# MLA heads: probabilities times values as three rounded products instead of one plain fp32 product

## The chip, the cores and the metric

The kernel runs on one core of a Trainium2 chip. The metric is the device time of one execution in microseconds (us); times in a trace count from the start of the profiled span. The engines are PE (TensorE, its weight loads as PEld), DVE (VectorE), ACT (ScalarE), POOL (GpSimd) and SP (SyncE, which only issues DMAs here). Each works through its own instructions in order; semaphores tie them together.

## What is computed

Two blocks over 1024 tokens at a width of 1024, all in fp32. The first block is not touched. The second has two layers, each with a pooling branch and an attention branch (MLA); the latter is what changes. Cut to that, with L = 1040 (16 learned tokens in front) and 8 heads:

```python
q = (c_q @ w_q_b).reshape(B, L, N_HEADS, QK_HEAD_DIM)
kv = (c_kv @ w_kv_b).reshape(B, L, N_HEADS, QK_NOPE_DIM + V_HEAD_DIM)
...
s = jnp.einsum('bqhd,bkhd->bhqk', q[:, q0:kend], k[:, :kend]).astype(jnp.float32) * scale
s = jnp.where(valid, s, MASK_VALUE)
p = jax.nn.softmax(s, axis=-1).astype(v.dtype)
outs.append(jnp.einsum('bhqk,bkhd->bqhd', p, v[:, :kend]))
```

## The kernel before

Activations lie transposed in SBUF, features on partitions and 1044 (padded) tokens along the free dimension, in 9 key tiles of 128. Large products are made of rounded fp32 (fp32r) operands: each operand is split into a high part, its rounded value, and a low part, what is left, and three products are added (high times high, high times low, low times high). POOL splits the weights as they stream in (L353, L362), DVE the activations.

The MLA heads take two stretches, 1868 to 2207 us for layer 0 and 2867 to 3205 for layer 1. The order is written out by hand: every engine runs the same loops, `for h in range(-1, MH)` over heads and `for n in range(NB)` over 15 slots, and does in slot n what its own code says ("slot 5" below means n = 5). PE works on head h (scores, products with values) and on the projections of head g = h + 1; iteration -1 has projections only, the last (h = 7) none.

- The queries fall into three pieces of 384, 384 and 276 columns (`pc`), the work of a head into 15 blocks (`BLOCKS`): 0 and 1 for the first piece, 2 to 6 for the second, 7 to 14 for the third. A block is one key tile by all queries of its piece, or two tiles (256 + 128, or 148 + 20 columns) at a diagonal. By width: seven blocks of 384, seven of 276, one of 168; 18 tiles per head.
- `scores(h, n)` (L803, mask L807): three rounded products per tile into one of two banks. It waits until the exponents of block n - 2 are done.
- `exponents(h, n)` on ACT (L1307): one instruction per block from PSUM into a ring of PRING = 6 plain fp32 slots, `prob(k)`, in `work`. A slot is free when the product that read it is done.
- `weigh_values(h, n - 2)` at the end of slot n on PE (L824): values (128 x 128, half of the columns ones, which gives the sums of the probabilities too) times probabilities, plain fp32, accumulated in `aux`. The profile shows a plain fp32 product as two matmuls.
- For the next head on PE: `key_value_part` (L692, slots 0, 5, 10), `query_part` (L708), `key_sum` (L720), `turn_values` (L741, slots 3, 8, 13), `query_sum` (L730, slots 4, 9, 14). All but query_part use one PSUM bank, `acc_n`, and wait until its last reader is through (`n_free`). ACT reads it in `key_value_evict` (L1238), `key_scale` (L1264), `values_in` (L932, slots 4, 9, 14; it copies the turned values out) and `query_scale` (L1275, slots 5, 10, and 0 of the next head).
- On DVE: `maximum` (L1846) takes row maxima of rough scores (PE L757 with mask L761, two banks in turn), `maxima_of` (L1851, or L1853 and L1854) joins them and `turn_maxima` on PE (L778, slots 0, 5, 10) turns them; `query_table` (L1812 to L1814, slots 4, 9, 14), `key_norm` (L1834 to L1838, slots 5, 10, and 0 of the next head) and `query_norm` (L1822 to L1826, slots 6, 11, and 1) make and split keys and queries. `rough_scores` of the next head (first in slots 7 and 12) need the query's high part from L1825. `head_out` (L1863, L1864, slots 3, 6, 10) scales the output.
- DVE sets up the ones beside the values ahead of the first head (L1869, L1870). In the last head it splits two finished rows (L1416, L1417, slots 7 and 8).

## Time and profile before

| | |
|---|---|
| median of 3 runs | 3358.72 us (3355.52 to 3359.7) |
| profiled execution | 3356.4 us, its span 3354.6 us |
| PE busy | 3057.1 us (91%), 16352 matmuls |
| DVE busy | 1440.9 us (43%) |
| ACT busy | 694.5 us (21%) |
| POOL busy | 1074.3 us (32%) |
| PE L803, scores | 864 matmuls, 208.4 us busy |
| PE L824, values | 576 matmuls, 177.3 us busy |
| ACT L1307, exponents | 240, 104.2 us busy |

Matmuls are pipelined and their busy times overlap; what a product takes of the time is read from the chain of waits, which follows the work back from the end and gives each piece of time to one instruction. In a timeline, brackets hold the time that the engine was idle before the instruction and who released it; "issue" is a release that the profile can't name.

### The profile page before, as it was taken

The numbers are of one execution on the slowest core, as the hardware profiler recorded it, in microseconds if no ns is written. First come the engines' busy times: TensorE is split into PE (matmuls) and PEld (weight loads), VectorE is DVE, ScalarE is ACT, GpSimd is POOL, SyncE is SP. The second block draws the span as 40 slices with busy tenths as digits, with TensorE's granted clock in tenths as the row PEclk, the third lists the DMA queues.
The fourth block names the chain that finished last, engine by engine and source line by source line (L and its number), as shares of the span: only waits on it lengthen the run. The fifth ranks groups of instructions, "written<-read, shape, count | busy, mean of one in ns | idle before, by whom it ended". The sixth has DMA issues, their size and how long they took to land.

```text
span 3354.6 us, 41151 instructions
## 1 busy us (share of the span) xinstructions
PE 3057.1 (91%) x16352; PEld 2688.7 (80%) x16352; DVE 1440.9 (43%) x1730; ACT 694.5 (21%) x1239; POOL 1074.3 (32%) x1335
## 2 busy tenths in 40 slices
PE   6976678899999997799999899989899999999999
PEld 4754556677788775699999788889899999788889
DVE  4678454422222223830011666671820111766661
ACT  2132320000000001100111455510100110455500
POOL 3523013344444443333333211133433432211132
PEclk9988789999999998899999999999899999999999
DMA  2101011111111111211212000051211212000042
GB/s 104 44 32 35 1 63 39 49 46 44 50 44 47 47 44 44 77 51 45 102 45 83 32 14 14 14 185 45 89 51 45 96 51 77 32 16 18 15 178 76
DMA packets 46429, 182.50 MB, mean 54 GB/s; under 512 B 5968, under 2 KB 6096, under 8 KB 45776
## 3 DMA queue, kind: packets, MB, share of 16 engines
q1 hardware_dynamic: 31248, 113.19, 10.6%
q10 hardware_dynamic: 15040, 67.28, 5.3%
q8 instruction: 107, 1.75, 0.2%
q14 instruction: 34, 0.28, 0.0%
HBM read 150.06 MB, written 30.39 MB: 54 GB/s over the span
## 4 chain that ended last, share of the span: by engine, by line
PE 80%; DVE 13%; ACT 3%; issue 2%; POOL 1%; DMA 0%; DVEq 0%; ACTq 0%; POOLq 0%; SPq 0%
PE acc L425 59%; PE aux L824 4%; PE acc L708 4%; PE acc L803 3%; DVE act_lo L1417 2%; PE acc L757 2%; PE acc L692 1%; DVE residual L1482 1%; DVE work L1433 1%; DVE work L1426 1%; PE acc L778 1%; DVE act_hi L1416 1%; PE acc L720 1%; POOL w_lo L353 1%; DVE residual L1505 1%
## 5 line engine op out<-in xcount | busy, mean ns | idle before, releaser
L425 PE MATMUL acc<-act_hi,w_hi 128*128 128x348 f32 (+1 forms) x3104 | 770.6, 349 | 100.7 <-DVE act_lo L1417 41.2
L353 POOL TENSOR_TENSOR w_lo<-w_raw,w_hi 128x256 fp32r<-128x256 f32 (+1 forms) x924 | 817.3, 916 | 17.2
L425 PE MATMUL acc<-act_lo,w_hi 128*128 128x348 f32 (+1 forms) x3104 | 763.9, 346 | 0.0
L425 PEld LDWEIGHTS acc<-act_hi,w_hi 128*128 128x128 f32 x3104 | 546.3, 191 | 162.4 <-issue 68.1
L425 PE MATMUL acc<-act_hi,w_lo 128*128 128x348 f32 (+1 forms) x3104 | 618.8, 345 | 0.0
L425 PEld LDWEIGHTS acc<-act_lo,w_hi 128*128 128x128 f32 x3104 | 548.8, 190 | 43.1
L425 PEld LDWEIGHTS acc<-act_hi,w_lo 128*128 128x128 f32 x3104 | 530.0, 189 | 42.1
L373 POOL TENSOR_TENSOR small<-shape_consts 128x1 f32<-128x1 f32 x192 | 40.9, 213 | 1607.0 <-PE acc L425 1607.0
L425 PE MATMUL acc<-ff_split,w_hi 128*128 128x512 f32 (+1 forms) x1408 | 317.7, 375 | 11.9 <-DVE ff_split L1417 11.9
L1634 DVE TENSOR_TENSOR residual<-acc,residual 128x1024 f32<-128x1024 f32 (+1 forms) x88 | 108.1, 1228 | 473.0 <-PE acc L425 472.9
L425 PEld LDWEIGHTS acc<-ff_split,w_hi 128*128 128x128 f32 x1408 | 253.0, 188 | 60.8 <-DVE ff_split L1417 16.5
L362 POOL CAST w_hi<-w_raw 128x1024 fp32r<-128x1024 f32 x23 | 25.8, 1122 | 632.6 <-PE acc L708 544.4
L1846 DVE TENSOR_REDUCE small<-acc 128x1 f32<-128x512 f32 (+4 forms) x240 | 132.1, 550 | 192.5 <-PE acc L761 121.9
L803 PE MATMUL acc<-ff_split 128*128 128x276 f32 (+5 forms) x864 | 208.4, 354 | 0.0
L374 POOL CAST w_hi<-w_raw 128x1024 fp32r<-128x1024 f32 x192 | 202.5, 1055 | 0.0
L824 PE MATMUL aux<-work 128*128 128x276 f32 (+5 forms) x576 | 177.3, 404 | 0.0
L425 PE MATMUL acc<-ff_split,w_lo 128*128 128x512 f32 (+1 forms) x704 | 166.8, 374 | 0.0
L803 PEld LDWEIGHTS acc<-ff_split 128*128 128x128 f32 x864 | 140.8, 190 | 31.3 <-ACT work L1307 0.5
L1138 ACT ACTIVATE work<-acc 128x1024 f32<-128x1024 f32 x32 | 32.7, 1027 | 627.0 <-PE acc L425 626.4
L932 ACT ACTIVATE work<-acc 64x384 f32<-64x384 f32 (+5 forms) x153 | 93.5, 620 | 289.2 <-PE acc L425 255.7
L1307 ACT ACTIVATE work<-acc 128x384 f32<-128x384 f32 (+2 forms) x240 | 104.2, 435 | 233.9 <-PE acc L803 160.6
L425 PEld LDWEIGHTS acc<-ff_split,w_lo 128*128 128x128 f32 x704 | 127.2, 188 | 22.5
(228 smaller groups left out, 3307.6 us busy)
## 6 DMA issues: line engine op xcount, KB each, us to landing
w_raw<-in_wstream SPq DMA_DIRECT2D x215, 512.0 KB, 3.5
spill_x<-residual ACTq DMA_DIRECT2D x2, 4176.0 KB, 12.2
spill_m<-residual ACTq DMA_DIRECT2D x2, 4176.0 KB, 12.6
spill_g<-work ACTq DMA_DIRECT2D x16, 522.0 KB, 2.7
residual<-spill_m ACTq DMA_DIRECT2D x16, 522.0 KB, 6.1
work<-spill_g ACTq DMA_DIRECT2D x16, 522.0 KB, 8.6
residual<-spill_x ACTq DMA_DIRECT2D x16, 522.0 KB, 4.3
residual<-in_xT ACTq DMA_DIRECT2D x8, 512.0 KB, 9.9
```

Of the source, the lines that this page charges most:

```text
L353: ins = nc.gpsimd.tensor_tensor(Wl[:, s, c0:c0 + w], Wraw[:, s, c0:c0 + w], Wh[:, s, c0:c0 + w].bitcast(F32), ALU.subtract)
L374: nc.gpsimd.tensor_copy(Wh[:, s, :], Wraw[:, s, :]).then_inc(sems["w_hi_done"], 1)
L425: ins = nc.tensor.matmul(acc[0:m, s, p, 0:w], wt[:, ws, w0 + j * m:w0 + j * m + m], x[:, k, p * w:p * w + w], start=(first and t == 0), st ...
L708: ins = nc.tensor.matmul(acc_q[:, 0:w], wt[:, w_head[0], j * P:j * P + P], x[:, j, c0:c0 + w], start=(j == 0 and t == 0), stop=(j == 5 and ...
L757: ins = nc.tensor.matmul(acc_r[bank][:, 0:n], qh[:, min(P * i, LASTQ):min(P * i, LASTQ) + P], kh[:, 512 * p:512 * p + n], start=True, stop ...
L803: ins = nc.tensor.matmul(out, k2[kt][:, c0:c0 + P], q2[qt][:, lo:lo + w], start=m == 0, stop=(m == 2 and not diag))
L824: ins = nc.tensor.matmul(aux[:, b % 2, lo - QP * pc:lo - QP * pc + w], values(h)[:, t, :], prob(k)[:, at:at + w], start=t == 0, stop=end)
L932: return nc.scalar.activation(out, in_, ACT.Copy, scale=scale)
L1307: do(nc.scalar.activation(prob(k)[:, 0:w], src, ACT.Exp), "p_in")
L1417: do(vec.tensor_tensor(lo, src, hi.bitcast(F32), ALU.subtract), name)
L1634: do(vec.tensor_tensor(x, acc_view(s, pieces), x, ALU.add), f"free{s}")
L1846: do(vec.tensor_reduce(S_[:, col:col + 1], acc_r[rough_bank(i, p)][:, 0:n], AX, ALU.max, negate=True), "rough_max")
```

## The change

- Probabilities and values move from `work` to rounded tiles (`pool_split`), each in two parts. The ring has 4 slots (PRING) instead of 6.
- ACT takes each exponent twice from the same scores: in fp32 into the slot of the low part (`prob32`), and rounded into the high part. The signal `p_hi` comes after the second.
- DVE subtracts the two (`low_probabilities`, block n - 1 at the start of slot n) in place over the fp32 value, and forms the low part of the values from PSUM (`low_part_values`, slots 4, 9, 14), which ends the use of the bank `acc_n` (`v_lo` in place of `v_in`, in `turn_values` too).
- PE makes three rounded products per tile instead of one plain one. It waits for `p_lo`; `scores` waits for `p_hi`.
- DVE clears the low parts beside the ones ahead of the first head (two more instructions per value buffer).

The diff, without the list of semaphores and two renamed waits on PE:

```diff
@@ -178,22 +178,27 @@
 
 
 
-        PRING = 6
+        PRING = 4
         QP = 3 * P
         NQP = -(-TP // QP)
 
-        def values(h):
-
-            o = 8 * RW + TB * P * (h % 2)
-            return R_[:, o:o + TB * P].rearrange("p (t c) -> p t c", c=P)
-
-        ring0 = 2 * TB * P
-
-        def prob(k):
-            o = 8 * RW + ring0 + QP * (k % PRING)
+        def values(h, part):
+
+            o = TB * P * (2 * (h % 2) + part)
+            return G_[:, o:o + TB * P].rearrange("p (t c) -> p t c", c=P)
+
+        ring0 = 4 * TB * P
+
+        def prob(k, part):
+            o = ring0 + QP * (2 * (k % PRING) + part)
+            return G_[:, o:o + QP]
+
+        def prob32(k):
+
+            o = 8 * RW + ring0 + QP * (2 * (k % PRING) + 1)
             return R_[:, o:o + QP]
 
-        idr0 = ring0 + QP * PRING
+        idr0 = ring0 + 2 * QP * PRING
         ident_r, causal_r, after_r = (G_[:, idr0 + P * i:idr0 + P * i + P] for i in range(3))
         extra0 = idr0 + 3 * P
         assert extra0 + QP <= 8 * RW
...
@@ -788,7 +793,7 @@
                     k = block_no(l, h, n)
                     pc, tiles = BLOCKS[n]
                     if k > 2:
-                        pe.wait_ge(sems["p_in"], k - 2)
+                        pe.wait_ge(sems["p_hi"], k - 2)
                     if tiles[0][0] == 0:
                         pe.wait_ge(sems["max_row"], wave(l, h, pc))
                         pe.wait_ge(sems["k_lo"], wave(l, h, pc))
...
@@ -816,13 +821,15 @@
                     if tiles[0][0] == 0:
                         if b > 2:
                             pe.wait_ge(sems[f"av_free{b % 2}"], (b - 1) // 2)
-                        pe.wait_ge(sems["v_in"], b)
-                    pe.wait_ge(sems["p_in"], k)
+                        pe.wait_ge(sems["v_lo"], b)
+                    pe.wait_ge(sems["p_lo"], k)
                     at = 0
                     for t, lo, w in tiles:
                         end = n in ENDS and t == tiles[-1][0]
-                        ins = nc.tensor.matmul(aux[:, b % 2, lo - QP * pc:lo - QP * pc + w], values(h)[:, t, :],
-                                               prob(k)[:, at:at + w], start=t == 0, stop=end)
+                        for m, (v, part) in enumerate(((0, 0), (0, 1), (1, 0))):
+                            ins = nc.tensor.matmul(aux[:, b % 2, lo - QP * pc:lo - QP * pc + w],
+                                                   values(h, v)[:, t, :], prob(k, part)[:, at:at + w],
+                                                   start=(t == 0 and m == 0), stop=(end and m == 2))
                         at += w
                     ins.then_inc(values_done(l, h, n)[0], 1)
 
...
@@ -1279,14 +1286,14 @@
 
                 def values_in(g, pc):
 
-                    v1 = values(g)
+                    v1 = values(g, 0)
                     act.wait_ge(sems["v_turned"], wave(l, g, pc))
                     if pc < NQP - 1:
                         do(copy(v1[:, 3 * pc:3 * pc + 3, 0:64],
-                                acc_n[:, 0:192].rearrange("p (t v) -> p t v", v=64)), "v_in")
+                                acc_n[:, 0:192].rearrange("p (t v) -> p t v", v=64)), "v_hi")
                     else:
                         do(copy(v1[:, 6:8, 0:64], acc_n[:, 0:128].rearrange("p (t v) -> p t v", v=64)))
-                        do(copy(v1[:, 8, 0:64], acc_n[:, 128:192], param("rows20")), "v_in")
+                        do(copy(v1[:, 8, 0:64], acc_n[:, 128:192], param("rows20")), "v_hi")
 
                 def maximum_row(h, pc):
 
...
@@ -1304,7 +1311,8 @@
                     if k > PRING:
                         back = k - 1 - PRING
                         act.wait_ge(*values_done(back // (NB * MH), back // NB % MH, back % NB))
-                    do(nc.scalar.activation(prob(k)[:, 0:w], src, ACT.Exp), "p_in")
+                    do(nc.scalar.activation(prob32(k)[:, 0:w], src, ACT.Exp))
+                    do(nc.scalar.activation(prob(k, 0)[:, 0:w], src, ACT.Exp), "p_hi")
 
                 def inverse_sums(h, pc):
 
...
@@ -1838,6 +1846,28 @@
                     do(vec.tensor_tensor(F[:, 4 * (g % 2) + K0 + 1, c0:c0 + w], key[:, 0:w], hi.bitcast(F32),
                                          ALU.subtract), "k_lo")
 
+                def low_probabilities(h, n):
+
+                    k = block_no(l, h, n)
+                    w = block_width(n)
+                    dve.wait_ge(sems["p_hi"], k)
+                    do(vec.tensor_tensor(prob(k, 1)[:, 0:w], prob32(k)[:, 0:w], prob(k, 0)[:, 0:w].bitcast(F32),
+                                         ALU.subtract), "p_lo")
+
+                def low_part_values(g, pc):
+
+                    v1, v2 = values(g, 0), values(g, 1)
+                    dve.wait_ge(sems["v_hi"], wave(l, g, pc))
+                    if pc < NQP - 1:
+                        do(vec.tensor_tensor(v2[:, 3 * pc:3 * pc + 3, 0:64],
+                                             acc_n[:, 0:192].rearrange("p (t v) -> p t v", v=64),
+                                             v1[:, 3 * pc:3 * pc + 3, 0:64].bitcast(F32), ALU.subtract), "v_lo")
+                    else:
+                        do(vec.tensor_tensor(v2[:, 6:8, 0:64], acc_n[:, 0:128].rearrange("p (t v) -> p t v", v=64),
+                                             v1[:, 6:8, 0:64].bitcast(F32), ALU.subtract))
+                        do(vec.scalar_tensor_tensor(v2[:, 8, 0:64], acc_n[:, 128:192], param("rows20"),
+                                                    v1[:, 8, 0:64].bitcast(F32), ALU.mult, ALU.subtract), "v_lo")
+
                 def maximum(h, i, p):
 
                     n = min(512, min(P * (i + 1), TP) - 512 * p)
...
@@ -1865,9 +1895,12 @@
 
                 dve.wait_ge(sems["g_spilled"], 64 * (l + 1))
                 for h in range(2):
-                    v1 = values(h)
+                    v1, v2 = values(h, 0), values(h, 1)
                     do(vec.tensor_copy(v1[:, 0:8, 64:128], ones[:, 0:64].unsqueeze(1).to_broadcast([P, 8, 64])))
                     do(vec.tensor_scalar(v1[:, 8, 64:128], ones[:, 0:64], param("rows20"), None, ALU.mult))
+                    do(vec.tensor_scalar(v2[:, 0:8, 64:128], ones[:, 0:64].unsqueeze(1).to_broadcast([P, 8, 64]),
+                                         0.0, None, ALU.mult))
+                    do(vec.tensor_scalar(v2[:, 8, 64:128], ones[:, 0:64], 0.0, None, ALU.mult))
                 do(vec.tensor_copy(ident_r, ident))
                 do(vec.tensor_copy(causal_r, C_[:, 384:512]))
                 do(vec.tensor_copy(after_r, C_[:, 512:640]))
...
@@ -1878,10 +1911,16 @@
                         dve.wait_ge(sems["g_spilled_late"], 64 * (l + 1))
                     for n in range(NB):
                         if h >= 0:
+                            if n:
+                                low_probabilities(h, n - 1)
+                            elif h:
+                                low_probabilities(h - 1, NB - 1)
                             if n == 0:
                                 key_norm(h, 2)
                             if n == 1:
                                 query_norm(h, 2)
+                        if more and n in (4, 9, 14):
+                            low_part_values(g, n // 5)
                         if more and n == 4:
                             query_table(g, 0)
                         if h >= 0:
...
@@ -1921,6 +1960,7 @@
                             if n in (7, 8) and not more:
                                 j = n - 7
                                 split(X[:, j, :], Fy[0][:, j, wide], Fy[1][:, j, wide], "f_ready")
+                low_probabilities(MH - 1, NB - 1)
                 head_out(MH - 1, 2)
                 do(vec.tensor_copy(S_[:, 40:41], S_[:, 60:61]), "to_act")
                 for j in range(2, 4):
```

DVE in slots 4 and 5 of a middle head, from the second maximum of slot 3 on (`acc` is PSUM, L1846 the maxima). Before:

```order
L1846 TENSOR_REDUCE small<-acc 128x1
L1812 TENSOR_TENSOR residual<-acc,work 128x384
L1813 COPY work<-residual 32x384
L1814 TENSOR_TENSOR residual<-residual,work 32x384
L1846 TENSOR_REDUCE small<-acc 128x1 x3
L1853 TENSOR_TENSOR small<-small 128x1
L1854 TENSOR_TENSOR small<-small 128x3
```

and now:

```order
L1876 TENSOR_REDUCE small<-acc 128x1
L1854 TENSOR_TENSOR pool_split<-work,pool_split 128x384
L1862 TENSOR_TENSOR pool_split<-acc,pool_split 128x3x64
L1820 TENSOR_TENSOR residual<-acc,work 128x384
L1821 COPY work<-residual 32x384
L1822 TENSOR_TENSOR residual<-residual,work 32x384
L1876 TENSOR_REDUCE small<-acc 128x1 x2
L1854 TENSOR_TENSOR pool_split<-work,pool_split 128x384
L1876 TENSOR_REDUCE small<-acc 128x1
L1883 TENSOR_TENSOR small<-small 128x1
L1884 TENSOR_TENSOR small<-small 128x3
```

Two subtractions for probabilities (L1854) and one for values (L1862) stand ahead of the joined maxima, L1884, which were L1854.

DVE in slots 9 to 11 of a head, from the last row of the query's table to the rounding of the query. Before:

```order
L1814 TENSOR_TENSOR residual<-residual,work 32x384
L1834 TENSOR_TENSOR residual<-work,residual 32x384
L1835 TENSOR_TENSOR residual<-residual 64x384
L1837 CAST ff_split<-residual 128x384
L1838 TENSOR_TENSOR ff_split<-residual,ff_split 128x384
L1863 TENSOR_TENSOR residual<-residual,work 64x384
L1864 TENSOR_TENSOR residual<-aux,residual 64x384
L1822 SCALAR_TENSOR_TENSOR residual<-residual,params 128x384
L1825 CAST ff_split<-residual 128x384
```

and now:

```order
L1822 TENSOR_TENSOR residual<-residual,work 32x384
L1854 TENSOR_TENSOR pool_split<-work,pool_split 128x276
L1842 TENSOR_TENSOR residual<-work,head_out 32x384
L1843 TENSOR_TENSOR residual<-residual,head_out 64x384
L1845 CAST ff_split<-residual 128x384
L1846 TENSOR_TENSOR ff_split<-residual,ff_split 128x384
L1893 TENSOR_TENSOR residual<-residual,work 64x384
L1894 TENSOR_TENSOR residual<-aux,residual 64x384
L1854 TENSOR_TENSOR pool_split<-work,pool_split 128x276
L1830 SCALAR_TENSOR_TENSOR residual<-residual,params 128x384
L1833 CAST ff_split<-residual 128x384
```

Two more subtractions, of 276 columns, stand ahead of the rounding (L1833, which was L1825).

PE at the end of slot 3 and in slot 4, from the products of a block of two tiles with the values (L824, now L830). Before:

```order
L824 MATMUL aux<-work 128x256
L824 MATMUL aux<-work 128x128
L803 MATMUL acc<-ff_split 128x384 x3
L757 MATMUL acc<-ff_split 128x512
L730 MATMUL acc<-residual,shape_consts 128x384
```

and now:

```order
L830 MATMUL aux<-pool_split 128x256 x3
L830 MATMUL aux<-pool_split 128x128 x3
L808 MATMUL acc<-ff_split 128x384 x3
L762 MATMUL acc<-ff_split 128x512
L735 MATMUL acc<-residual,shape_consts 128x384
```

Only the products with the values differ: three in the place of each.

## Rows read from the trace of the kernel before

**Rows 1.** Busy by stretch: from:to length, PE, PEld, DVE, ACT, POOL, clock, DMA, GB/s

```profile
1868.00:2207.00 339.00, 325.17 (x1881) 271.59 (x1880) 221.95 (x447) 185.64 (x417) 40.98 (x77) 0.99 0.07 23
1980.00:2020.00 40.00, 39.26 (x232) 33.06 (x230) 25.83 (x53) 22.21 (x52) 4.46 (x9) 1.00 0.04 13
2867.00:3205.00 338.00, 325.58 (x1883) 272.25 (x1882) 221.97 (x447) 185.45 (x417) 40.83 (x77) 1.00 0.07 23
```

**Rows 2.** Chain of waits inside 1868 to 2207, its shares by line

```profile
by line: PE aux L824 20.3%; PE acc L708 20.3%; PE acc L803 16.6%; PE acc L757 7.9%; PE acc L692 7.1%; PE acc L778 4.9%; PE acc L720 4.3%; PE acc L730 2.9%; issue 2.5%; PE acc L741 2.3%; PE acc L807 1.7%; PE acc L761 1.5%; ACT residual L1275
```

**Rows 3.** Chain of waits, one head: start us, us, what

```profile
1990.73 0.65 PE aux L824 x2
1991.38 0.53 PE acc L803 x3
...
2009.21 0.47 PE aux L824 x2
2009.67 0.38 PE acc L803 x3
...
2016.05 0.28 PE acc L803 x3
```

**Rows 4.** Timeline of PE, same head: start us, us, engine, line, what [idle before]

```profile
1993.21 0.64 PE L778 MATMUL acc<-shape_consts,small 128*1 128x128 f32 x6
...
1997.53 0.22 PE L757 MATMUL acc<-ff_split 128*128 128x128 f32 x1
...
2005.63 0.40 PE L692 MATMUL acc<-act_hi,w_hi 128*128 128x276 f32 x1 [0.40 <-ACT residual L1275]
...
2010.39 0.47 PE L757 MATMUL acc<-ff_split 128*128 128x512 f32 x1 [0.34 <-issue]
...
2016.56 0.68 PE L730 MATMUL acc<-residual,shape_consts 128*128 128x276 f32 x2
```

**Rows 5.** Timeline of DVE, same head

```profile
1981.26 0.45 DVE L1826 TENSOR_TENSOR ff_split<-residual,ff_split 128x276 fp32r<-128x276 f32 x1
1983.26 0.69 DVE L1846 TENSOR_REDUCE small<-acc 128x1 f32<-128x512 f32 x1 [1.55 <-PE acc L757]
...
1988.49 0.69 DVE L1846 TENSOR_REDUCE small<-acc 128x1 f32<-128x512 f32 x1 [0.22 <-PE acc L761]
...
1992.46 0.16 DVE L1853 TENSOR_TENSOR small<-small 128x1 f32<-128x1 f32 x1
1992.65 0.17 DVE L1854 TENSOR_TENSOR small<-small 128x3 f32<-128x3 f32 x1
...
1994.42 0.56 DVE L1838 TENSOR_TENSOR ff_split<-residual,ff_split 128x384 fp32r<-128x384 f32 x1
...
1996.83 0.36 DVE L1825 CAST ff_split<-residual 128x384 fp32r<-128x384 f32 x1
...
2003.81 0.56 DVE L1846 TENSOR_REDUCE small<-acc 128x1 f32<-128x384 f32 x1 [2.46 <-PE acc L761]
...
2009.93 0.36 DVE L1825 CAST ff_split<-residual 128x384 fp32r<-128x384 f32 x1
...
2015.29 0.69 DVE L1846 TENSOR_REDUCE small<-acc 128x1 f32<-128x512 f32 x1 [1.32 <-PE acc L757]
```

**Rows 6.** Timeline of ACT, same head

```profile
2002.51 0.32 ACT L932 ACTIVATE work<-acc 128x192 f32<-128x192 f32 x1
```

**Rows 7.** Timeline of ACT, last head: two exponents with no wait between

```profile
2199.82 0.69 ACT L1307 ACTIVATE work<-acc 128x276 f32<-128x276 f32 x2
```

**Rows 8.** Timeline of PE, last head, its wait in slot 5

```profile
2192.81 0.64 PE L778 MATMUL acc<-shape_consts,small 128*1 128x128 f32 x6 [0.82 <-DVE small L1854]
```

**Rows 9.** Timeline of DVE, before the first head and at its first query

```profile
1859.06 1.25 DVE L1417 TENSOR_TENSOR act_lo<-work,act_hi 128x1044 fp32r<-128x1044 f32 x1
...
1867.60 1.97 DVE L1417 TENSOR_TENSOR act_lo<-work,act_hi 128x1044 fp32r<-128x1044 f32 x1
...
1876.51 0.56 DVE L1812 TENSOR_TENSOR residual<-acc,work 128x384 f32<-128x384 f32 x1 [3.12 <-ACT residual L1254]
```

8 lines of the change are left out of this document (4 added, 4 removed).

## Prediction

> **What bounds the kernel now.** I read busy time by stretch first, then the chain of waits, then the timelines of one head. The two stretches in which the MLA heads run are 339 and 338 us long, and PE is busy for 325 us of either; inside layer 0, PE is busy 39.26 of 40 us, DVE 25.83, ACT 22.21, POOL 4.46, at granted clock 1.00, the 2.4 GHz level [rows 1]. In the chain nearly all of this stretch lies on PE lines: L824, the line that the change rewrites, has 20.3%, L803, the scores with the same tiles, 16.6%, and time that no engine was busy for is 2.5% [rows 2]. So PE sets the pace, but in order and with little slack: it already stops for DVE or ACT at three places, 0.34 and 0.40 us in a middle head [rows 4] and 0.82 us in the last [rows 8].
>
> **What PE gains.** 288 plain-fp32 products (two passes each, 576 matmuls) become 864 rounded ones of the same widths. For a 384-column tile the pair takes 0.65 us of the chain and three rounded products 0.53; for 276 columns 0.47 and 0.38; three products of 20 columns take 0.28, so the narrow tiles pay for their loads [rows 3]. As L803 is exactly such a set, the whole gain is the difference of the shares: 3.7% of 339 = 12.5 us per layer, 25 in all, 1.6 per head [rows 2].
> The Trainium skill (VectorE: DVE Perf Modes, The TRN2 errata) gives a matmul max(60, 6 + columns) cycles of 2.4 GHz; a 20-column one would be 0.025 us where this trace has 0.093 [rows 3]. By it the 16 such tiles would be 3 us cheaper in all.
>
> **What DVE gets, per head.** One subtraction per block, seven of 384 columns, seven of 276 and one of 168, plus three on values. The same form (SBUF minus SBUF to a rounded tile) takes 0.56 at 384 and 0.45 at 276, and neighbours stand 0.03 apart [rows 5], so 0.59 and 0.48 each. Those on values read PSUM; no such row exists. By the two rows' slope (0.11 per 108 columns) 192 columns are 0.36, 0.39 with the step; the bounds are zero and the 0.59 of 384 columns. The last third, two instructions, I take at 0.6. Sum: 7 x 0.59 + 7 x 0.48 + 0.36 + 2 x 0.39 + 0.6 = 9.2 us per head on an engine that has 14 idle in 40 [rows 1]. On average it fits. But DVE works in order, in bursts, and PE waits at the end of each burst. So I follow the bursts slot by slot, in shifts against the times of before (+1.2 is 1.2 us later), in a head whose neighbours are alike.
>
> 1. Slots 3 to 5. From the maximum at 1988.49 DVE runs without a pause to L1854, which ends at 1992.82; PE turns the maxima at 1993.21 [rows 4, 5]. The burst now also holds the low parts of block 3, of the values' first third and of block 4: 0.59 + 0.39 + 0.59 = 1.57. L1854 then ends at 1994.3 (PE came 0.1 earlier, by its cheaper products), PE follows some 0.1 behind, as 2010.39 follows the end of the cast at 2009.93 [rows 4, 5]. PE's shift: +1.2. The stop for the low values ahead of the query sum, and the one for the bank of rough(8,2), lie inside this.
> 2. Slots 6 and 7. The burst goes on to the query's rounding, which ended at 1997.19 for a product at 1997.53 [rows 4, 5]. Block 5 adds 0.59: it ends at 1997.19 + 1.57 + 0.59 - 0.1 = 1999.25. PE's shift: +1.75.
> 3. Slots 7 to 9. PE gains 0.15; the next burst starts at 2003.81 + 1.6.
> 4. Slots 9 to 12. That burst ended at 2010.29 and PE started 0.10 later after a stop of 0.34 [rows 4, 5]. Two 276-column subtractions stand in it (blocks 9 and 10): +0.96, nothing to absorb it. PE's shift: 1.6 + 0.96 = +2.55.
> 5. Slots 12 to 14. PE gains 0.17. The query sum at 2016.56 [rows 4] now waits for the last low values. DVE's maximum ended at 2015.98 [rows 5]; with 2.4 of shift, 0.48 for block 13 and 0.6 for values it ends at 2019.5 against PE's 2018.95. PE's shift: +3.0.
> 6. Slots 0 to 2. DVE has 1.55 of idle before 1983.26 [rows 5], and the three subtractions there take 0.36 + 0.59 + 0.59: it just fits, PE stops for none. Wide blocks gain 0.1 to 0.2, and the block of 148 and 20 columns gives that back.
>
> That is 2.8 us per head, with 0.2 off for the gains of 6. Fourteen heads (0 to 6, twice) have this form: 39 us. In the last head of a layer there is no projection to hide DVE, and PE waited for it already [rows 8]: the subtractions of blocks 1 to 4 are 2.4 us less about 0.4 of idle, so +2.0 each, and later slots, with two wide splits on DVE, hold it there. Before the first head the low values come ahead of the query's first instruction, which ends an idle stretch of 3.12 us [rows 9]: 0.4 for the work and some 0.2 for the wait on ACT, and 0.4 once more at the second third: 1.0 each. The constants added ahead (two of 512 and two of 64 columns) have no row of their own form; from 0.56 at 384 [rows 5] and 1.25 at 1044 columns [rows 9] they are at most 3 us together, and lie in that idle 3.12; were it shorter, the excess would add in full.
> **Sum:** 39 + 4 + 2 = 45 us. The profiled execution took 3356.4 us, so 3401.6; its own time is 2.3 under the median of the runs shown, and I forecast 3402.
>
> **ACT.** The second exponent needs no wait behind the first; two 276-column ones in a row take 0.69, not 0.80, so each adds 0.29 [rows 7], at 384 columns about 0.38: 5 us per head on 22 of 40. It costs where PE waits for ACT: the 0.40 at 2005.63 [rows 4] grows by 0.3 to 0.4. In the walk this lies between steps 3 and 4 and is covered, since DVE ends later (2.55 of shift). The low values wait for ACT's copy, which ended 0.98 before the maximum behind them (2002.51 + 0.32 to 2003.81) [rows 5, 6]: no cost there. The ring of four blocks instead of six: a block's exponent waits for the product of four blocks before, which PE issues two slots earlier; nothing in the middle heads, part of the 2.0 in the last.
>
> **Rivals.**
> *The gain comes through.* PE loses nothing to DVE because the subtractions fall into DVE's idle time, as the averages say. Its place is the ends of the two bursts (steps 1 and 4), and it decides where each has over 1.5 us of slack, against the 0.4 and the none that [rows 4, 5] show. Then 3356.4 - 25 + 4 (ACT's 0.3 in 14 heads) = 3335. Against it: the stop of 0.34 at 2010.39 is there without the change.
> *The bursts absorb half.* If DVE overlaps neighbours as ACT does (0.1 each) [rows 7], and maxima that waited are then ready at once, a head costs 1.3 to 1.8 instead of 2.8: 3356.4 + 14 x 1.5 + 5 = 3382.
> *POOL in DVE's way.* DVE's subtraction over 1044 columns takes 1.25 alone and 1.97 in the stretch before the first head, where POOL rounds weights beside it [rows 9]; in the heads POOL is busy 4.46 of 40 us, one in nine [rows 1]. If one in nine of the added 9.2 us takes 1.6 times as long, it is 0.6 per head, 9 in all: 3410. The Trainium skill (GPSIMD Engine Reference, the table at its head) has GpSimd's SBUF interface shared with VectorE when the latter has two SBUF inputs, which the new subtraction has. The rows agree with it as far as they go; the worst this rule would do here is those 9 us.
> *No gain on PE.* If the rounded products at this place ran no faster than the pairs, steps 3, 5 and 6 lose their gains, 0.5 to 0.8 per head: 3402 + 10 = 3412.
>
> **How the numbers follow.** Forecast 0.65; half absorbed 0.14; POOL or no gain together 0.11; gain comes through 0.08; a balance of both within 0.2% 0.02. A measurement tells 0.2%, 7 us, from no change. Slower: 0.65 + 0.14 + 0.11 = 0.90, less 0.01 for the low end of the half-absorbed case: 0.89; same 0.03; faster 0.08. For the range, the cost per head goes from 1.5 (overlap, no stop at step 5) to 3.7 (subtractions at 1.2 times their price, the low values at 0.59), and the last heads and starts together from 2 to 8: 3356.4 + 23 = 3379 and 3356.4 + 60 = 3416. I take 3378 to 3418, which holds all but the case in which the gain comes through.
>
> **What would show it.** Right: PE idle of 10% or more in the heads' stretches, each near 361 us long; as releasers of PE's idle time DVE's maxima and query casts (L1854 and L1825 now, L1884 and L1833 in the changed kernel), about 1 us each per head; DVE busy near 80% there (222 + 9.2 x 8 of 361); the chain passing from PE to DVE and back; the new value products at no more than 17% of the chain. Wrong: PE still busy 98% with stretches under 330 us (the gain came through); waits on ACT's exponents ahead of those on DVE; a second subtraction form that takes well over 0.56.

## The result, and the profile after

The changed kernel takes 3436.03 us (median of 4 runs, 3430.32 to 3437.7), the kernel before 3357.12 beside it (3354.86 to 3359.7). The ratio is 1.0232, with an interval from 1.0214 to 1.025: slower by 79 us where I had forecast 45, and outside the range of 3378 to 3418. The profiled executions took 3430.32 and 3356.4 us, 73.9 apart; the sums below are made against that difference.

The page of the changed kernel, its parts 1 and 4 in part:

```profile
PE 3062.1 (89%) x16640; PEld 2710.1 (79%) x16640; DVE 1579.7 (46%) x2042; ACT 773.8 (23%) x1479; POOL 1075.4 (31%) x1335
...
PE 74%; DVE 17%; ACT 5%; issue 4%; POOL 1%; DMA 0%; DVEq 0%; ACTq 0%; POOLq 0%; SPq 0%
```

Busy by stretch, with the columns of [rows 1], and the shares by line in the chain of waits over the same 339 us:

```profile
1868.00:2207.00 339.00, 298.57 (x1824) 256.00 (x1825) 261.26 (x545) 205.30 (x487) 34.77 (x66) 0.99 0.04 13
...
2000.00:2040.00 40.00, 35.93 (x231) 31.61 (x230) 30.86 (x65) 24.05 (x59) 4.60 (x9) 1.00 0.04 14
```

```profile
by line: PE acc L713 14.2%; PE aux L830 12.1%; PE acc L808 11.4%; issue 8.9%; DVE small L1876 6.2%; PE acc L762 5.1%; PE acc L697 4.9%; PE acc L783 4.6%; PE acc L725 4.3%; ACT pool_split L1315 3.3%; DVE pool_split L1854 3.3%; PE acc L746 2.
```

TensorE was busy in 39.26 of 40 us [rows 1] and is now in 35.93, at a granted clock of 1.00 in both, the 2.4 GHz level; VectorE rose from 25.83 to 30.86. The chain leaves TensorE for VectorE's maxima (L1876), its subtractions (L1854), ScalarE's rounded exponent (L1315), and 8.9% of "issue" where it was 2.5% [rows 2].

TensorE's stops in one middle head, which begins at 1985.65 (the counterpart of [rows 4], where the head begins at 1977.27):

```profile
1996.23 0.40 PE L746 MATMUL acc<-shape_consts,work 64*128 64x64 f32 x3 [0.30 <-ACT residual L1271]
...
1998.95 0.91 PE L735 MATMUL acc<-residual,shape_consts 128*128 128x384 f32 x2 [0.35 <-DVE pool_split L1862]
...
2003.24 0.49 PE L783 MATMUL acc<-shape_consts,small 128*1 128x128 f32 x3 [0.47 <-DVE small L1884]
...
2008.16 0.30 PE L762 MATMUL acc<-ff_split 128*128 128x128 f32 x1 [0.69 <-issue]
...
2016.76 0.40 PE L697 MATMUL acc<-act_hi,w_hi 128*128 128x276 f32 x1 [0.76 <-ACT residual L1282]
...
2022.19 0.47 PE L762 MATMUL acc<-ff_split 128*128 128x512 f32 x1 [1.18 <-issue]
...
2029.23 0.73 PE L735 MATMUL acc<-residual,shape_consts 128*128 128x276 f32 x2 [0.59 <-DVE pool_split L1868]
```

VectorE in that head, the operations that TensorE came for or that stand in front of them:

```profile
1998.53 0.36 DVE L1862 TENSOR_TENSOR pool_split<-acc,pool_split 128x192 fp32r<-128x192 f32 x1
...
2002.93 0.16 DVE L1884 TENSOR_TENSOR small<-small 128x3 f32<-128x3 f32 x1
...
2007.70 0.36 DVE L1833 CAST ff_split<-residual 128x384 fp32r<-128x384 f32 x1
...
2008.69 0.56 DVE L1854 TENSOR_TENSOR pool_split<-work,pool_split 128x384 fp32r<-128x384 f32 x1
...
2012.07 0.45 DVE L1854 TENSOR_TENSOR pool_split<-work,pool_split 128x276 fp32r<-128x276 f32 x1
```

The maxima are done at 2003.09 and TensorE turns them at 2003.24; the query is rounded by 2008.06 and the rough product goes at 2008.16. Those are the ends of bursts that the prediction followed. The stop marked "issue" at 2022.19 is the same: the cast L1833 had ended at 2022.09. One kind of stop was not in the walk: at 1996.23, for ScalarE's scaled keys. It comes back in slot 13 (0.26 us); in slot 8 the profile shows no idle time, but the turn of the values begins 1.38 us behind the start of the projection ahead of it, and 1.19 once the scaled keys go first. The stop at 2029.23, for the last low values, was in the walk, at 0.55.

ScalarE just before the first of them, in the changed kernel:

```profile
1994.69 0.49 ACT L1314 ACTIVATE work<-acc 128x384 f32<-128x384 f32 x1 [1.49 <-PE acc L808]
1995.08 0.49 ACT L1315 ACTIVATE pool_split<-acc 128x384 fp32r<-128x384 f32 x1
1995.59 0.58 ACT L1271 ACTIVATE residual<-acc,small 128x384 f32<-128x384 f32 x1
```

The second exponent begins 0.39 us behind the first and pushes the scaled keys back by that; TensorE waits for them to turn the values.

The last head of layer 0, TensorE's longest stops, and what stands on VectorE ahead of the second:

```profile
2225.59 0.64 PE L783 MATMUL acc<-shape_consts,small 128*1 128x128 f32 x6 [1.54 <-DVE small L1884]
...
2232.03 0.62 PE L830 MATMUL aux<-pool_split 128*128 128x276 f32 x3 [1.25 <-DVE pool_split L1854]
...
2234.44 0.65 PE L830 MATMUL aux<-pool_split 128*128 128x276 f32 x3 [1.41 <-DVE pool_split L1854]
```

```profile
2230.16 1.25 DVE L1425 TENSOR_TENSOR ff_split<-residual,ff_split 128x1044 fp32r<-128x1044 f32 x1
2231.43 0.45 DVE L1854 TENSOR_TENSOR pool_split<-work,pool_split 128x276 fp32r<-128x276 f32 x1
```

The subtraction that TensorE waits for at 2232.03 stands behind one of the two wide splits; the next one stands behind the other.

Where the time went, from such timelines. The times are from a head's first key and value product to TensorE's work named; the shifts stand beside those of the prediction's steps.

| station | before | after | shift | forecast |
|---|---|---|---|---|
| turn of maxima, slot 5 (step 1) | 15.94 | 17.59 | 1.65 | 1.2 |
| rough product, slot 7 (step 2) | 20.26 | 22.51 | 2.25 | 1.75 |
| key and value product, slot 10 (from step 3) | 28.36 | 31.11 | 2.75 | 1.6 |
| rough product, slot 12 (step 4) | 33.12 | 36.54 | 3.4 | 2.55 |
| query sum, slot 14 (step 5) | 39.29 | 43.58 | 4.3 | 3.0 |
| next head (after step 6) | 40.86 | 45.12 | 4.3 | 2.8 |

The neighbouring head lengthens from 40.80 to 44.95, so a head costs 4.2. The pass before the first head goes from 31.14 to 33.69 us in layer 0 (2.55, forecast 1.0). The last head, from its first turn of maxima to the next part of the layer, goes from 22.9 to 28.1 (5.2, forecast 2.0). Fourteen heads, two starts and two last heads are 59 + 5 + 10 = 74 us. That this is the difference of the two profiled executions is in part luck. Measured from the first key and value product to the next part of the layer, the stretch goes from 339.2 to 377.6 us in layer 0 and from 338.1 to 376.4 in layer 1, together 77. The 3 above the sum lie in short pieces of the changed kernel's trace with a lower granted clock (0.66 from 2163 to 2168, 0.72 from 2914 to 2920, 0.83 from 3262 to 3272), and outside the two stretches that trace is 3 us shorter than the one before.

### The profile page after: what moved, and what is told of

It reads as the page before. It is cut to its first block, busy times and chain, and to the rows that moved or that the text cites. A ratio compares the mean times of both kernels' runs of the same rounds, so it can differ in the third digit from the quotient of the medians.

```text
span 3428.5 us, 42569 instructions
## 1 busy us (share of the span) xinstructions
PE 3062.1 (89%) x16640; PEld 2710.1 (79%) x16640; DVE 1579.7 (46%) x2042; ACT 773.8 (23%) x1479; POOL 1075.4 (31%) x1335
## 4 chain that ended last, share of the span: by engine, by line
PE 74%; DVE 17%; ACT 5%; issue 4%; POOL 1%; DMA 0%; DVEq 0%; ACTq 0%; POOLq 0%; SPq 0%
PE acc L430 58%; PE acc L713 3%; PE aux L830 3%; PE acc L808 2%; DVE act_lo L1425 2%; DVE small L1876 2%; DVE residual L1490 1%; DVE work L1441 1%; PE acc L762 1%; DVE work L1434 1%; PE acc L697 1%; DVE pool_split L1854 1%; PE acc L783 1%; DVE act_hi L1424 1%; PE acc L725 1%
## 5 line engine op out<-in xcount | busy, mean ns | idle before, releaser
L830 PE MATMUL aux<-pool_split 128*128 128x276 f32 (+5 forms) x864 | 174.3, 319 | 5.9 <-DVE pool_split L1854 5.9
L1876 DVE TENSOR_REDUCE small<-acc 128x1 f32<-128x512 f32 (+4 forms) x240 | 132.1, 550 | 101.1 <-PE acc L766 56.8
L808 PE MATMUL acc<-ff_split 128*128 128x276 f32 (+5 forms) x864 | 163.3, 302 | 0.0
L830 PEld LDWEIGHTS aux<-pool_split 128*128 128x128 f32 x864 | 131.6, 190 | 29.5 <-issue 8.5
L1680 DVE TENSOR_TENSOR work<-work 128x1024 f32<-128x1024 f32 x32 | 40.4, 1262 | 243.6 <-ACT work L1145 243.4
L1434 DVE TENSOR_TENSOR work<-work 128x1044 f32<-128x1044 f32 (+1 forms) x47 | 65.1, 1385 | 175.9 <-ACT work L951 174.8
```

Source lines behind the costliest of these rows:

```text
L808: ins = nc.tensor.matmul(out, k2[kt][:, c0:c0 + P], q2[qt][:, lo:lo + w], start=m == 0, stop=(m == 2 and not diag))
L830: ins = nc.tensor.matmul(aux[:, b % 2, lo - QP * pc:lo - QP * pc + w], values(h, v)[:, t, :], prob(k, part)[:, at:at + w], start=(t == 0 a ...
L1434: do(vec.tensor_tensor(total, total, slots[1 + j % 2][:, cols], ALU.add), "sum_ready" if j == n - 1 else "sq_free" if j <= n - 3 else "dve ...
L1876: do(vec.tensor_reduce(S_[:, col:col + 1], acc_r[rough_bank(i, p)][:, 0:n], AX, ALU.max, negate=True), "rough_max")
```

## The experiments

Ratios are to the kernel before, run on the same chip, with their 95% intervals; its medians there were 3354.4 to 3356.1 us. "Minus" is against the changed kernel's 3436.0 unless said otherwise. That kernel was measured beside 3357.1, so by the ratios the same differences come out 2 to 4 us smaller, and each is known to about 6 us; what a head takes in the traces is the finer measure.

**Second exponent left out.** The fp32 exponent is dropped and VectorE subtracts the high part from itself, so the low parts of the probabilities are zero.

```diff
-                    do(nc.scalar.activation(prob32(k)[:, 0:w], src, ACT.Exp))
```

> Left out: the fp32 copy of the exponent (ScalarE takes each exponent once, rounded; VectorE subtracts it from itself in the same number of instructions, so the low parts are zero). Read from the trace of the changed kernel: behind the second exponent stands the key scale (L1271), which the turning of the values (L746) waits for in slots 3, 8 and 13, 0.2 to 0.3 us each, and the query scale (L1282). Theory 'two engines' (VectorE's bursts and ScalarE's second exponent both cost): 0.8 to 1.1 us per head less, 12 to 18 us with the last heads, so 3418 to 3424 against 3436. Theory 'VectorE alone', as the prediction had it: 3434 to 3436.

Measured: 3418.18 us, ratio 1.019 (1.0173 to 1.0207), minus 18. The theory of two engines gave that; ScalarE's exponents were not covered.

**Low parts of the probabilities left out.** The subtraction is dropped, and the products read the high part in its place.

```diff
-                                low_probabilities(h, n - 1)
...
-                                low_probabilities(h - 1, NB - 1)
...
-                                                   values(h, v)[:, t, :], prob(k, part)[:, at:at + w],
+                                                   values(h, v)[:, t, :], prob(k, 0)[:, at:at + w],
```

> Left out: the 15 subtractions per head that make the low parts of the probabilities (all three products read the high part). Prediction's term: 2.15 + 0.96 + 0.48 us of burst per head less 0.5 of slack, some 3.0 per head, 42 us in 14 heads, and 6 to 8 in the last heads: 3386. If the loss came from ScalarE or from the products, at most 10 us go: above 3425.

Measured: 3372.0 us, ratio 1.0049 (1.0032 to 1.0065), minus 64 where 50 was expected. A head falls from 45.0 to 41.7 us: 3.3 x 14 = 46. The last head of layer 0 takes 22.4 us where it took 28.1, which is 11 more in the two. One subtraction per block carries most of the loss.

**Low parts of the values left out.** The products read the values' high part.

```diff
-                        if more and n in (4, 9, 14):
-                            low_part_values(g, n // 5)
...
+                                                   values(h, 0)[:, t, :], prob(k, part)[:, at:at + w],
```

> Left out: the low parts of the values (four instructions on VectorE per head, and the wait of the query sum for them; all three products read the high part). Theory 'two engines': the stops ahead of the query sum in slots 4 and 14, 0.35 and 0.6 us, and those before the first head, 2 us: 14 x 1.0 + 4 = 18 us less, 3418. If they only fill a gap that the probabilities' subtractions leave anyway: 3430 or more.

Measured: 3410.67 us, ratio 1.0163 (1.0146 to 1.018), minus 25. A head falls by 1.2 to 43.8, in 14 heads 17 us, and the pass before the first head loses its three waits for low values, 2.5 us in each layer. That is 7 us more than was expected of four small instructions: TensorE waits for their ends in slots 4 and 14 (0.35 and 0.59 us), and they stand ahead of the maxima.

**One product of three in the changed kernel.** Two rounded products of each tile are left out, everything else stays.

```diff
-                        for m, (v, part) in enumerate(((0, 0), (0, 1), (1, 0))):
+                        for m, (v, part) in enumerate(((0, 0),)):
```

> Left out: two of the three products per tile on TensorE (the low parts are made and waited for, not used). Per head 36 matmuls fewer, 4.7 us of TensorE by the scores' price. Theory 'TensorE sets nothing in the bursts': it gives back only what lies between the bursts (slots 7 to 9, 12 to 2), a third to a half, 1.6 to 2.4 us per head: 3398 to 3412. If TensorE were the bound throughout, 75 us less: 3361.

Measured: 3419.45 us, ratio 1.0193 (1.0176 to 1.021), minus 17, less than any case expected. TensorE's stops took over what its work gave up: the waits at the rough products of slots 7 and 12 are 1.41 and 1.74 us here, 0.69 and 1.18 with all three products. In the changed kernel VectorE's bursts set the pace, and an engine that waits at their ends gains little from doing less.

**The products alone.** One exponent, no low parts; all three rounded products read the high parts, so both corrections are left out.

```diff
-                    do(nc.scalar.activation(prob32(k)[:, 0:w], src, ACT.Exp))
...
-                                low_probabilities(h, n - 1)
...
-                            low_part_values(g, n // 5)
...
+                                                   values(h, 0)[:, t, :], prob(k, 0)[:, at:at + w],
```

> Left out: the second exponent and all low parts; three rounded products of the high parts stay. It isolates the product step against the plain one of the kernel before. Prediction: 25 us less than before, 3330 to 3334. Rival 'no gain on TensorE' (three rounded products take as long as the pair): 3355.

Measured: 3346.1 us (9 runs), ratio 0.997 (0.996 to 0.998): 10 us below the kernel before, where 25 were expected. The chain of waits over the same stretch, by line:

```profile
by line: PE acc L713 20.3%; PE aux L830 17.7%; PE acc L808 16.8%; PE acc L762 8.1%; PE acc L697 7.2%; PE acc L783 4.9%; PE acc L725 4.3%; PE acc L735 2.9%; issue 2.9%; PE acc L746 2.3%; PE acc L812 1.7%; PE acc L766 1.5%; ACT residual L1282
```

The value products' share went from 20.3% [rows 2] to 17.7%, and not to the 16.6% of the scores that I had equated them with. Single pieces of that chain:

```profile
1992.01 0.72 PE aux L830 x3
...
1994.69 0.53 PE aux L830 x3
...
2000.16 0.83 PE aux L830 x6
...
2007.10 0.39 PE aux L830 x3
```

Three products of 384 columns take 0.53 behind a projection but 0.72 behind the turn of the maxima. The pair of before takes 0.65 and 0.84 in the same two places, so the 0.19 of the change-over stays. There are three such places in a head, and the scores never stand there. The two blocks cut in 256 and 128 columns gain next to nothing (0.83 for 0.85), and the block with 148 and 20 columns takes 0.57 where its four plain passes took 0.38.

**The products alone, reordered** by the moves of the reordered kernel before, below, which leave TensorE no stop. The corrections are left out as above.

```diff
+                        if h >= 0 and n in (5, 10):
+                            inverse_sums(h, n // 5 - 1)
...
+                        if more and n in (3, 8, 13):
+                            key_scale(g, n // 5)
...
+                            if n in (6, 11):
+                                head_out(h, n // 5 - 1)
```

> The products alone (one exponent, no low parts; all three rounded products read the high parts, so the corrections are left out), with ScalarE's and VectorE's work in the order of the reordered kernel before. That kernel runs at 3335.6 us and TensorE has no stop in its middle heads, so here the gain of the products on TensorE is seen with nothing to give it back. If the gain is the 8 us per layer by which the share of the value products in the chain fell in the run of the products alone: 3335.6 - 16 = 3320 (3317 to 3323). If it is the 25 us of the prediction and waits on other engines hid it: 3311 (3308 to 3314). If only the 10 us of that run's total are there: 3326 (3324 to 3328).

Measured: 3327.71 us, ratio 0.9915 (0.9899 to 0.9932). That is 7.9 below the reordered kernel before (3335.63), near the lowest of the expected gains. TensorE has no stop in the middle heads of either, and a head takes 38.93 us against 39.64: 0.7. So the missing 15 us did not hide behind waits. Over four heads' chain the value products take 8.0 instead of 9.1 us per head, a gain of 1.1 where I claimed 1.6, and 0.36 of that comes back in the pieces of other products (L808 0.14, L762 0.13, L697 0.09). Why those grow stays open. The products gain 8 to 10 us in all.

**Scaled keys ahead of the exponents** on ScalarE, in slots 3, 8 and 13; same arithmetic.

```diff
+                        if more and n in (3, 8, 13):
+                            key_scale(g, n // 5)
                         if h >= 0:
                             exponents(h, n)
...
-                                key_scale(g, n // 5)
```

> The changed kernel with one move on ScalarE: the key scale of slots 3, 8 and 13 stands ahead of the exponents of its slot. Theory 'the second exponent costs where the turning of the values waits for the key scale': three waits of 0.25 us per head go, 10 to 14 us less, 3422 to 3426. If the exponent's cost (18 us by the run that left it out) lies at the query scale or in the scores' wait: 3432 or more.

Measured: 3421.53 us, ratio 1.0199 (1.0182 to 1.0216), minus 14.5. TensorE turns the values without a stop and a head takes 44.1 us. Leaving the exponent out gave 44.2. So nearly all that the second exponent costs is its place in ScalarE's queue.

**Subtractions of the probabilities on GpSimd,** in all but the last head of a layer. The waits and the order of GpSimd's weight splits follow.

```diff
+                nc.gpsimd.tensor_tensor(prob(k, 1)[:, 0:w], prob32(k)[:, 0:w], prob(k, 0)[:, 0:w].bitcast(F32),
+                                        ALU.subtract).then_inc(sems["p_lo"], 1)
```

> The subtractions of the probabilities' low parts go from VectorE to GpSimd in all heads but the last, between the pieces of its weight split. By its 0.92 us for 256 columns a block takes 1.0 to 1.4 us there, 17 us per head beside 4.5 us of weights. Theory 'bursts on VectorE': nearly what leaving them out gave in the middle heads, 56 of 64 us, less 0 to 10 for the later p_lo and for both engines reading SBUF at once: 3380 to 3390. Theory 'any added wait of TensorE for a low part costs': 3400 or more.

Measured: 3433.83 us, ratio 1.0237 (1.022 to 1.0254): within noise of the changed kernel, 44 to 54 us over what was expected. Timeline of GpSimd, then of VectorE, in this run:

```profile
1999.13 1.02 POOL L376 TENSOR_TENSOR pool_split<-work,pool_split 128x384 fp32r<-128x384 f32 x1 [2.11 <-ACT pool_split L1339]
...
2002.13 1.01 POOL L376 TENSOR_TENSOR pool_split<-work,pool_split 128x384 fp32r<-128x384 f32 x1 [1.24 <-ACT pool_split L1339]
...
2006.92 1.01 POOL L376 TENSOR_TENSOR pool_split<-work,pool_split 128x384 fp32r<-128x384 f32 x1 [3.38 <-ACT pool_split L1339]
2007.89 0.77 POOL L421 TENSOR_TENSOR w_lo<-w_raw,w_hi 128x128 fp32r<-128x128 f32 x1
...
2009.49 0.78 POOL L421 TENSOR_TENSOR w_lo<-w_raw,w_hi 128x128 fp32r<-128x128 f32 x1
```

```profile
1999.30 1.26 DVE L1846 TENSOR_TENSOR residual<-residual,work 32x384 f32<-32x384 f32 x1
...
2002.26 0.89 DVE L1908 TENSOR_TENSOR small<-small 128x1 f32<-128x1 f32 x1
...
2006.34 0.55 DVE L1919 TENSOR_TENSOR residual<-aux,residual 64x384 f32<-64x384 f32 x1
2006.93 1.42 DVE L1854 SCALAR_TENSOR_TENSOR residual<-residual,params 128x384 f32<-128x384 f32 x1
...
2009.98 0.29 DVE L1901 TENSOR_REDUCE small<-acc 128x1 f32<-128x128 f32 x1
...
2017.01 0.55 DVE L1846 TENSOR_TENSOR residual<-residual,work 32x384 f32<-32x384 f32 x1
```

L1846 takes 0.55 us with GpSimd still and 1.26 beside its subtraction: it begins 0.17 later and ends 0.41 after GpSimd's end. L1854 (the query's norm here) takes 1.42 beside a subtraction and a weight split, 0.62 in the changed kernel. The joining of the maxima, L1908, takes 0.89 where the changed kernel has 0.16, and TensorE waits for it. A maximum from PSUM, L1901 at 2009.98, takes its 0.29 with GpSimd at work beside it. Between 1960 and 2160 VectorE is busy 146.4 us with 255 instructions, in the changed kernel 155.5 with 323. It lost a fifth of its instructions and 6% of its time. A head takes 45.4 us, against 45.0. The Trainium skill (GPSIMD Engine Reference, the table at its head) has the two share an SBUF interface when VectorE reads two SBUF inputs; these rows agree, and they give the size.

**The same, with scaled keys first.**

```diff
+                        if more and n in (3, 8, 13):
+                            key_scale(g, n // 5)
```

> Both moves together. With VectorE's bursts short again ScalarE's waits show in full: 12 to 16 us under the run with GpSimd alone, 3366 to 3378. Still over the kernel before, by the low values' 20 us.

Measured: 3422.75 us, ratio 1.0201 (1.0184 to 1.0218), the time of the scaled keys alone, where 3366 to 3378 was expected. The move to GpSimd is worth nothing with or without ScalarE's stop.

**Subtractions at the end of the slot,** behind its other work, not at its start.

```diff
-                            if n:
-                                low_probabilities(h, n - 1)
...
                             if n == 10:
                                 head_out(h, 1)
+                            if n:
+                                low_probabilities(h, n - 1)
```

> The changed kernel with the same instructions; on VectorE the low part of block n - 1 stands at the end of slot n instead of its start, so the maxima, the key and query norms of the slot go first. Theory 'it is the place in the burst, not VectorE's load': one block fewer ahead of the joined maxima and of either query's rounding, and none ahead of the low values: 0.5 us at each of three stations, 1.0 to 1.6 us per head, 14 to 22 us less, 3413 to 3421. Theory 'VectorE's load': no change, 3436.

Measured: 3436.44 us, ratio 1.0243 (1.0226 to 1.026): no change, where 15 to 23 us less were expected. Timeline of VectorE in this run, ahead of the first low values of a head that begins at 1989.63:

```profile
2001.19 0.69 DVE L1876 TENSOR_REDUCE small<-acc 128x1 f32<-128x512 f32 x1 [0.58 <-PE acc L766]
2001.92 0.56 DVE L1854 TENSOR_TENSOR pool_split<-work,pool_split 128x384 fp32r<-128x384 f32 x1
2002.51 0.36 DVE L1862 TENSOR_TENSOR pool_split<-acc,pool_split 128x192 fp32r<-128x192 f32 x1
```

The low values begin 12.88 us after the head's start, as in the changed kernel (1998.53 less 1985.65). Between them and the last moment when VectorE was idle stand the same maximum and one subtraction; only which block it belongs to has changed. A subtraction at the end of slot 3 stands just where that of the start of slot 4 stood, so the queue is the same but for the block, and every station of the head stands within 0.03. In slot 12 TensorE now stops 0.83 us for a subtraction instead of 1.18 for the rough product behind it, and that product goes at the same time.

**Reordered:** subtractions last, scaled keys first, inverse sums behind the query's scale on ScalarE (slots 5 and 10), the head's output behind the query's norm on VectorE (slots 6 and 11). Same arithmetic as the change.

```diff
+                        if h >= 0 and n in (5, 10):
+                            inverse_sums(h, n // 5 - 1)
...
+                            if n in (6, 11):
+                                head_out(h, n // 5 - 1)
```

> The same, with three more moves: the key scale ahead of the exponents (15 us by its own run), the inverse sums of pieces 0 and 1 behind the query scale of slots 5 and 10, the scaling of the output behind the query norm of slots 6 and 11. Each of the last two takes about 1.0 to 1.1 us out of a chain that PE waits for. If the waits are in series, 14 + 15 + 14 x 1.5 = 50 us less: 3380 to 3392. If one of them hides the others: 3400 to 3410.

Measured: 3399.54 us, ratio 1.0133 (1.0116 to 1.015), minus 36.5: of the expected size, 7 us short of its range. The stops at both rough products and for the query's scale are gone (a head takes 42.65); what stays is TensorE waiting for VectorE itself, here three of five stops in a middle head:

```profile
1994.30 0.91 PE L735 MATMUL acc<-residual,shape_consts 128*128 128x384 f32 x2 [0.35 <-DVE pool_split L1861]
...
1998.60 0.64 PE L783 MATMUL acc<-shape_consts,small 128*1 128x128 f32 x6 [0.48 <-DVE small L1883]
...
2014.32 0.65 PE L830 MATMUL aux<-pool_split 128*128 128x276 f32 x3 [0.51 <-DVE pool_split L1853]
```

The last is new: a subtraction that stands behind the longer work of its slot is now itself late for its product.

**Reordered, without the second exponent** (the low parts of the probabilities are zero).

```diff
-                    do(nc.scalar.activation(prob32(k)[:, 0:w], src, ACT.Exp))
```

> The reordered changed kernel without the exponent in full fp32 (the low part becomes zero, so that correction is left out); VectorE's subtractions stay. If the second exponent cost 18 us only through the place in which it stands, ahead of the scaled keys, then with the scaled keys ahead of it there is next to nothing left to win: 3399.5 - 2 = 3397 (3394 to 3400). If it costs by its length wherever it stands, since ScalarE's values reach VectorE and TensorE that much later: 3381 to 3388.

Measured: 3398.03 us, ratio 1.0126 (1.011 to 1.0143): 1.5 below the reordered kernel, where the same removal gave 18 in the changed one. The exponent costs by its place and not by its length.

**The kernel before, reordered** by the same moves but for the subtractions, which it doesn't have.

```diff
+                        if h >= 0 and n in (5, 10):
+                            inverse_sums(h, n // 5 - 1)
...
+                        if more and n in (3, 8, 13):
+                            key_scale(g, n // 5)
...
+                            if n in (6, 11):
+                                head_out(h, n // 5 - 1)
```

> The kernel before with the three moves that need no low parts (key scale, inverse sums, output scaling). Its own stops are 0.40 us at the query scale of slot 10, 0.34 at the query's rounding of slot 12 and up to 0.2 at each turning of the values: 0.8 to 1.0 us per head, 11 to 14 us less, 3342 to 3346. If these stops only pass to another engine: 3350 or more.

Measured: 3335.63 us, ratio 0.9944 (0.9928 to 0.9961), 20 us below the kernel before and 6 below the expected range. It beats both kernels at the arithmetic of before. Its busy times over the stretch of [rows 1]:

```profile
1868.00:2207.00 339.00, 329.21 (x1924) 278.03 (x1925) 227.01 (x453) 188.62 (x417) 40.35 (x76) 0.99 0.10 33
```

The two stops of [rows 4], 0.40 and 0.34 us, are gone and a head takes 39.64 us for 40.83. That is 1.2 for 0.74 of stops. The remaining 0.45 stands at the same two places. The scores and the projection behind them in slot 10, in the kernel before and then reordered:

```profile
2004.49 0.74 PE L803 MATMUL acc<-ff_split 128*128 128x276 f32 x3
...
2005.63 0.40 PE L692 MATMUL acc<-act_hi,w_hi 128*128 128x276 f32 x1 [0.40 <-ACT residual L1275]
```

```profile
2000.13 0.74 PE L803 MATMUL acc<-ff_split 128*128 128x276 f32 x3
...
2000.71 0.39 PE L692 MATMUL acc<-act_hi,w_hi 128*128 128x276 f32 x1
```

From start to start it is 1.14 us with the stop and 0.58 without: 0.56 for a stop of 0.40. Where nothing holds it, a product begins 0.16 us ahead of the end shown for the one before it, and a stop takes that overlap too. In slot 12 it is 1.09 and 0.58, 0.51 for a stop of 0.34, and the product behind the stop takes 0.09 more.

**A single rounded product** (one exponent, no low parts, both corrections left out: a lower precision than either kernel). It is the edit of the products alone, and:

```diff
-                        for m, (v, part) in enumerate(((0, 0), (0, 1), (1, 0))):
+                        for m, (v, part) in enumerate(((0, 0),)):
```

> Left out: all low parts, the second exponent and two of the three products, so probabilities and values are rounded once. The products then take about a third of the 60 us of the chain per layer: 80 us of TensorE less than the run with three products alone (3346). With TensorE free, the waits for VectorE and ScalarE that are short now grow; by the run with one product in the changed kernel (a fifth of its TensorE time came through) and that with three products alone (two fifths), 25 to 50 us come through: 3296 to 3321.

Measured: 3308.17 us, ratio 0.9858 (0.9841 to 0.9874). This lies inside the expected range. Two rounded products fewer than in the run of the products alone are 38 us. That is less than what they take, for TensorE's stops in a middle head grow from 1.0 to 2.9 us, 27 in 14 heads. The price is better read from the chain of the two reordered kernels without stops: 9.1 us per head for the plain products and 8.0 for three sets of rounded ones, 2.7 a set, so a plain product costs some 3.4 rounded ones.

## Why the prediction was wrong in size and right in kind

- **What bounds the kernel:** held. TensorE paces the kernel before, in order and without slack, and the change turns VectorE's time into TensorE's stops. The marks of kind held: idle above 10% (40.4 of 339 us), releasers L1884 and L1833 (named "issue"), VectorE at 77%, value products at 12.1% of the chain. Those of size did not: the stretches are 377.6 and 376.4 us long where 361 was said, and the stops per head are 0.5 for L1884 and 1.9 for L1833 where it was about 1 each.
- **"What PE gains", 25 us:** failed by its size. Measured 10 alone, and 8 with no stops. The step that failed is "L803 is exactly such a set": it is one of widths, but not of places. Of 1.6 per head, 0.5 never comes, since the scores' share has none of the three change-overs, and 0.36 comes back in other products. The walk used only 0.6 to 0.8 per head of the claimed 1.6, so little of this went into the forecast; the run of the products alone gives 0.5 per head.
- **"What DVE gets", prices:** held. The subtractions took 0.56 and 0.45, the values' 0.36 as sloped from [rows 5].
- **Steps 1 and 2:** right in place, 0.45 and 0.5 short. 0.36 of either is ScalarE's stop at the turn of the values in slot 3, which the scaled-keys run removes (turn of maxima at 17.23). The wait for the low values was said to "lie inside" the burst. It does: without them the turn of maxima comes only 0.38 earlier.
- **"ACT", no cost:** failed. I looked only where TensorE waited for ScalarE already (slot 10) and found that covered. The scaled keys of slots 3, 8 and 13 stand behind the exponents in the same queue, and their slack was shorter than the 0.39 added. Leaving the exponent out gave 18 us, scaled keys first 14.5, and leaving it out of the reordered kernel 1.5. This is 0.9 of the 1.4 us per head by which the walk was short; of the other 0.5 the runs name no single cause. The ring of four blocks was said to cost nothing in the middle heads, which holds: in layer 0 the profile of the changed kernel shows no exponent waiting for a product with the values. No run took the ring back to six.
- **Step 4:** right in mechanism. The stop in slot 12 is 1.18 where it was 0.34, and the shift there grows from 2.75 to 3.4. That is 0.65 where 0.96 was added with "nothing to absorb it"; the wait for ScalarE in slot 10 had grown from 0.40 to 0.76 and took the difference. With the second exponent left out the two stops are 0.5 and 1.48.
- **Step 5:** right in place, 1.3 short, of which 0.96 is again ScalarE's: with scaled keys first the query sum comes at 42.62 instead of 43.58.
- **Last heads, 2.0 each:** 5.2 measured in layer 0. The walk took the work of blocks 1 to 4 and stopped there; from the first turn of maxima to the second it is 13.1 us for 11.3, so 1.8 of the 2.0. The three stops for L1854 in the later slots, together 3.0 us, were left to the clause on the two wide splits and not priced.
- **Starts, 1.0 each:** 2.55 measured in layer 0. The three query sums came 0.46, 0.46 and 1.36 us later behind the turn of the values than before, and the walk had only the first two.
- **Rivals:** the gain does not come through, half is not absorbed, and TensorE's gain exists. POOL in VectorE's way cost next to nothing as the change is written: the longest of the 240 subtractions of probabilities took 0.56 us. As a mechanism it is real and large, once GpSimd is given the work.

In sum 20 us of the excess of 29 lie in the middle heads (1.4 x 14), 6 in the last heads and 3 in the starts, by the sizes of layer 0. Another 5 us of the 79 lie between the profiled execution and the median of its kernel. The range was too narrow because its upper end priced one engine's spread and not the engine that I had called free.

## What to carry to other kernels

- In a kernel whose engines work in order, a new instruction is priced by who waits for what stands behind it in its own queue, and not by the engine's average load. For each one, list the consumers of the next three results in that queue and their slack. ScalarE was busy for 22 of 40 us, and 0.39 us in the wrong place still cost 0.9 us a head.
- Look for the order first. Moving three pieces of work gained 20 us in the kernel before, more than the 8 to 10 that the products gave, and with the subtractions some 35 in the changed one.
- A move within a queue counts only if it passes an instruction for which the engine waits or that another engine waits for.

## What the runs showed of the hardware

- On SBUF tiles GpSimd and VectorE took turns rather than working side by side: a 384-column subtraction on GpSimd took 1.01 us, and VectorE's two-input operation of 0.55 beside it 1.26, one of a single column 0.89 for 0.16, and a rounding copy with one SBUF input 0.94 for 0.36 (at 2018.76). VectorE's operations that read PSUM kept their time (0.29, and 0.56 for 384 columns).
- A stop of TensorE cost 0.16 to 0.17 us more than the idle time shown, 0.56 for 0.40 and 0.51 for 0.34, since it also takes the overlap of the products on either side.
- Plain fp32 products cost about 3.4 times a rounded one over this mix of widths. The narrow tiles are the exception: the 148 and 20 column pair went from 0.38 to 0.57 us when four plain passes became six rounded ones.
- The same three products take 0.53 or 0.72 us, by what stands ahead of them on TensorE, and the plain pair shows the same step of 0.19.
